# Two more products of 128x512 at the end of each step of the second experts

## The reference

```
scores = sigmoid(xf @ w_router); choice = scores + b_router
keep the 4 best of 8 groups, then the 6 best of the 64 experts for each token
gate = scores of the chosen, divided by their sum, x 2.5
for each expert e, on its tokens:  hb = silu(xb @ w_gate[e]) * (xb @ w_up[e])
                                   y  = (hb @ w_down[e]) * gate
routed[token] += y;   output = shared expert + routed
```

## Time and profile before

| | us |
|---|---|
| median of 3 runs | 1918.8 |
| profiled execution | 1919.48 |
| its span | 1917.4 |
| TensorE busy | 1645.2 (86%) |
| VectorE busy | 630.7 (33%) |
| ScalarE busy | 458.2 (24%) |
| GpSimd busy | 478.3 (25%) |

### The profile page before, as it was taken

The page is one execution under the profiler, slowest core; times in us unless marked ns, Lnnn a source line. Parts: engine busy times, 40 slices in busy tenths (PEclk is TensorE's granted clock), DMA queues, the critical chain, the costliest instruction groups (busy, mean ns, idle before and its releaser), DMA issues. The chain is left out here.

```text
span 1917.4 us, 22063 instructions
## 1 busy us (share of the span) xinstructions
PE 1645.2 (86%) x8000; PEld 905.6 (47%) x8000; DVE 630.7 (33%) x1602; ACT 458.2 (24%) x984; POOL 478.3 (25%) x385
## 2 busy tenths in 40 slices
PE   6989999899999968999999969979877887877880
PEld 3434446773333326678778756444333333323330
DVE  1775516441111106651644234512111111111115
ACT  2412216321111105652642122111111110101111
POOL 4997907001111106740200000012111111111100
PEclk9799999989999988999999979989898998889895
DMA  5353410548999954412212265458999999999954
GB/s 197 132 186 110 157 63 5 220 169 340 405 406 404 402 151 144 173 64 88 94 45 88 92 238 197 174 178 311 397 384 377 379 376 353 368 368 399 355 180 139
DMA packets 112343, 446.23 MB, mean 233 GB/s; under 512 B 20356, under 2 KB 26900, under 8 KB 74856
## 3 DMA queue, kind: packets, MB, share of 16 engines
q1 hardware_dynamic: 96360, 411.13, 55.0%
q0 software_dynamic: 15840, 33.60, 7.0%
q10 hardware_dynamic: 32, 0.04, 0.0%
HBM read 427.33 MB, written 44.10 MB: 246 GB/s over the span
## 5 line engine op out<-in xcount | busy, mean ns | idle before, releaser
L1993 PE MATMUL bank<-big,heads 128*32 128x512 f32 (+2 forms) x944 | 259.4, 659 | 47.5 <-DMA big<-in_w_exp_up_dram 41.6
L1993 PEld LDWEIGHTS bank<-big,heads 128*32 128x32 f32 (+2 forms) x944 | 81.8, 140 | 147.6 <-issue 147.1
L2044 DVE SCALAR_TENSOR_TENSOR heads<-heads,small,bank 128x256 f32<-128x256 f32 x39 | 18.7, 480 | 391.2 <-ACT heads L2096 391.2
L2283 POOL DMA_INDIRECT acc_scratch<-heads,small x55 | 87.2, 1586 | 231.4 <-DVE heads L2076 131.6
L460 PE MATMUL bank<-big,h_cols 128*128 128x512 f32 x320 | 143.3, 602 | 0.3 <-ACT heads L610 0.3
L2124 POOL DMA_INDIRECT heads<-h_scratch,small x39 | 40.4, 1035 | 379.6 <-DVE small L2061 341.6
L1993 PE MATMUL bank<-h_cols,heads 128*32 128x512 f32 (+1 forms) x256 | 80.5, 687 | 34.1 <-DMA big<-in_w_exp_up_dram 34.1
L1175 PE MATMUL bank<-causal,ident 128*128 128x512 f32 x178 | 92.9, 671 | 15.6 <-PEq L178 15.6
L2029 PE MATMUL bank<-h_rows,heads 128*32 128x512 f32 (+2 forms) x336 | 103.4, 613 | 0.6 <-ACT heads L2090 0.6
L2096 ACT ACTIVATE heads<-bank 128x256 f32<-128x256 f32 x39 | 15.0, 384 | 370.8 <-PE bank L1993 370.8
L818 POOL TENSOR_SCALAR junk_and_spare<-junk_and_spare,cond 128x512 f32<-128x512 f32 x56 | 97.4, 1740 | 5.5
(11 more groups left out here) (476 smaller groups left out, 3199.3 us busy)
## 6 DMA issues: line engine op xcount, KB each, us to landing
big<-in_w_exp_gate_dram SPq DMA_DIRECT2D x65, 1024.0 KB, 16.3
big<-in_w_exp_up_dram SPq DMA_DIRECT2D x65, 1024.0 KB, 26.8
h_rows<-in_w_exp_down_dram SPq DMA_DIRECT2D x40, 1024.0 KB, 25.1
big<-in_w_in_dram SPq DMA_DIRECT2D x13, 2048.0 KB, 8.7
junk_and_spare<-in_w_mod_dram SPq DMA_DIRECT2D x24, 1024.0 KB, 5.4
big<-in_w_exp_down_dram SPq DMA_DIRECT2D x24, 1024.0 KB, 20.8
junk_and_spare<-in_w_exp_gate_dram SPq DMA_DIRECT2D x16, 1024.0 KB, 19.0
junk_and_spare<-in_w_exp_up_dram SPq DMA_DIRECT2D x16, 1024.0 KB, 30.5
```

The source lines that it names most:

```text
L1993: mm = pe.matmul(b_au[b][tile, :], xt[:, b, P * c + tile.start:P * c + tile.stop], gu[places[n][0]][:, :, c, :], start=c == 0, stop=c == K ...
L2283: return pool.indirect_dma_start(out=acc, out_offset=bass.IndirectOffsetOnAxis(at, 0), in_=rows, in_offset=None, bounds_check=acc.shape[0] ...
```

## The change

At the end of each i that has both a current and a previous step, directly behind the down product and its increment of `y_mm`, TensorE issues two more products of the identity with the constant tile, into bank 5. Nothing reads them: the next thing written to that bank is the next turn of hidden rows. No wait, load or other engine is changed.

```
                     mm.then_inc(y_mm, 1)
+                    if has(i, 0):
+                        keep_clock(K, pe, b_ht, 2)
```

## The result

The changed kernel takes 1926.3 us (median of 9 runs, 1923.21 to 1930.32), the kernel before 1920.6 us (9 runs): 5.7 us more by the medians. The ratio is 1.0034, 95% interval 1.0020 to 1.0048, which is 6.5 us (3.8 to 9.2). The forecast was 1925 in a range of 1914 to 1940, and +5.7 us by its sum. The two profiled executions stand closer together (1919.48 and 1923.21 us), because the one after was the fastest of its nine; so I compare them stretch by stretch.

The account below looks back on a forecast made before the run. TensorE was taken to be late in the early steps, the loads from step 7 on, TensorE's chain at the end. The terms 6.84 + 1.71 - 0.85 - 2 = 5.7 us on 1919.5 gave 1925, range 1914 to 1940.

Parts of the forecast that it names:

- The first steps, +6.84 us: Steps 1 to 8: later down products delay load issue; until down(4) ends this costs 4 x 1.71 us, afterwards nothing.
- the prediction's sign was 5 to 6: Second experts' stage: the last wait for weights would end 5 to 6 us later than in the kernel before.
- Lateness in the middle, 0 us: Steps 9 to 36: loads issued late enter a queue that still has work, so 0, at most 12 us.
- late issues pass on: Rival, chance 0.20: late loads open a hole in each of seven middle rounds, 12 us more, ending at 1940.
- The clock in the middle, -2 us: Middle gate and up: shorter waits keep the full clock in some steps, 2 us gained (bounds 0 and 19).
- one or two hundredths: Sign in the middle: clock rises from 0.90 by this much, while waits for weights fall from 89 to some 50 us.
- all nine: The nine long middle waits before gate and up: would stay at 3.6 us and more, so lose the full clock.
- 19 us of holes: Middle part: DMA engines' idle share, 0.04 x 478.5 us, taken as all that faster TensorE work could win.
- Both rivals that rested on the clock (1917 and 1907): Middle: clock regained, 11.4 us reach the end (1917, chance 0.16); or all 19 us of holes close (1907, 0.06).
- The clock of the last gate and up, -0.85 us: Behind the last wait for weights (3.17 us): keeping the full clock would gain 1.7 us; half was taken.
- The end, +1.71 us: After the last weight loads: products behind down(36) delay gate and up of 38, down(37) and its scatter by 1.71 us.
- the place at i = 38: Products of step 38 delay only the last down product, whose scatter waits for the one before anyway: 0 us.

Follow-up runs that it names:

- places 1 to 5: Changed kernel with the two products only behind the down products of steps 0 to 4 (i from 1 to 5): ratio 1.0043 to the kernel before.
- 5 to 8: Changed kernel with the two products only for i = 5 to 8: ratio 0.9994 to the kernel before.
- 32 places: Changed kernel with the two products only for i from 6 to 37: ratio 1.0006 to the kernel before, +1.2 us.
- The run with four products: Changed kernel with four products instead of two in all 38 places: ratio 1.0068 to the kernel before, +13.0 us.
- the paddings: Two runs of the kernel before with 76 tiny or 152 short products added behind the last down product: ratios 1.0005 and 0.9987.
- the run with the new order and two products: Kernel before with gate and up loads no longer queued behind the previous slot's down load, plus two products in all 38 places: ratio 1.0027.
- last +0.2: Changed kernel with the two products only at i = 38, behind the down product of step 37: ratio 1.0001 to the kernel before.

## Why the prediction was right

**The first steps, +6.84 us: right.** Down(4) ends 6.87 us later, the DMA share before it falls, and the runs with places 1 to 5 (+8.2 us) and 5 to 8 (-1.2 us) show both sides of the border that the step drew: the first moment from which the queue has work without a break. The last wait for weights ends 7.3 us later in the span, 6.7 from down(0), where the prediction's sign was 5 to 6.

**Lateness in the middle, 0 us: right.** 32 places there leave the stretch at 506.4 us. The rival that ended at 1940, late issues pass on, is out for two products. Four make the stretch 1.4 to 2.2 us longer, which may be the first sign of it.

**The clock in the middle, -2 us: wrong in size, and in its reason.** More came back than I had said (0.91 to 0.95, not one or two hundredths; waits of 42 us, not 50), and the stretch got 0.15 us shorter, which is nothing. Two steps of the reasoning failed. It took 1.71 us off each wait, while the lateness adds up over the steps between two waits: the first long wait shrank by 6.6 us and kept the full clock, which the prediction had ruled out for all nine. And it took up to 19 us of holes as something that a faster TensorE could close. The run with four products has 0.99 of the clock, a fifth of the waits (17.2 of 89 us) and a DMA share of 0.97, as the paddings have with none (0.97). So the missing 3 to 4 hundredths of the share do not close with TensorE's clock, as long as fillers raise it. What a full clock without fillers would give was not tested. Both rivals that rested on the clock (1917 and 1907) fall for this change.

**The clock of the last gate and up, -0.85 us: -1.7.** The wait fell from 3.17 to 1.95 us and the step took 7.07 us instead of 8.77. There, with no loads left, it counted in full, as the step said.

**The end, +1.71 us: right**, and nothing for the place at i = 38.

**Not in the prediction: -3.2 us** from TensorE's branch. By the profiled pair the terms make 6.87 - 0.15 - 1.7 + 1.7 - 3.2 = 3.5 us, and 0.4 us less stands in the table: 0.6 us less between down(37) and the last add, and small amounts the other way behind it.

The pair does not carry the whole measured difference. By the medians it is +5.7 and by the ratio 6.5 us, with an interval from 3.8; the pair's 3.1 us from down(0) to the end, or 3.7 with what lies ahead of the stage, are just below it. Where the other 3 us are no trace shows. What lies ahead of the stage varies by more than that, and the changed kernel may not have the short branch in every execution: the run with the new order and two products has the same TensorE program and a branch of 3.79 us. Which of the two it is stays open.

That the sum of 5.7 met the median is partly luck. Three terms were off: 2 us of clock gain in the middle that did not come, 0.85 us more of it at the end than I had taken, and 3.2 us of branch in the profiled execution. The last two pull against the first. The single runs agree with the account, within wide intervals: first places +8.2, middle +1.2, last +0.2 make 9.6 us, the whole change made 6.5, and none of the three single runs has the short branch (it takes 3.40, 3.83 and 3.88 us there).

## What to carry to other kernels

In a stage that ping-pongs between an engine and a load queue, find the first moment from which the queue always has work: what is added to the engine before it costs its full time, what is added behind it costs nothing as long as waits for data take the lateness up (two products per step here; with four the stretch began to grow). Do not count on the clock that such fillers bring back: it paid here where the engine's chain alone was left, behind the last load, and in the middle it did not show in the length of the stretch. And an edit that adds instructions moves code: look at the branches behind it before the difference is put down to the work.

## What the runs showed of the hardware

In the profiled executions TensorE's branch over the overflow code took 3.4 to 4.0 us in the kernel before and in seven of the experiments, and 0.46 us in the changed kernel, with four products, and with both paddings; nothing in between. The count of packets on the instruction queue (68 before, 69 after) does not tell the cases apart: the run with the middle places has 69 as well. The Trainium skill, "Runtime: NRT & Kernel Launch", section "Instruction fetch mechanics", says that code is fetched in blocks of 256 instructions and that a taken branch to a block that is not there waits for the fetch. The trace agrees in kind: 304 instructions more (152 products and as many weight loads) shorten it and 256 more, in the run with the middle places, do not. But the run with the new order of loads and two products has these 304 too, in the same TensorE program, and a branch of 3.79 us:

```profile
L2189 PEldq COMPARE_BRANCH  x2: 382/2086/3791, 714.9 to 1897.8; - x2
```

So the length of this code alone does not decide. What else does was not tried, and that the long branch waits for a fetch is not shown either.
